# A network kernel of two blocks: the attention jobs of its last two layers start early and in another order, each with one dense tile beside it

## What is computed

```python
u = x * (1 + scale) + shift
h = split_cols(u @ w_in)                 # 27 feature tiles and 6 token tiles
o_dsa = dsa_mixer(rope(dsa_q), rope(dsa_k), dsa_v, rope(idx_q), rope(idx_k), idx_w)
o_fox = fox_mixer(fox_q, fox_k, fox_v, log_sigmoid(fox_f + b_f))
kc, vc = nsa_compress(...)               # silu(blocks @ w1) @ w2
o_nsa = nsa_mixer(nsa_q, rope(nsa_q), kc, vc, rope(ks), vs, rope(kw), vw, sigmoid(nsa_g))
mix = concatenate([o_dsa, o_fox, o_nsa])
y = (mix * silu(gate)) @ w_out
x = layer_norm(ALPHA * x + (1 + gate_c) * y, ln_g, ln_b)
```

## Time and profile before

| | |
|---|---|
| median of 3 runs | 1975.18 us (1973.48 to 1976.91) |
| span of the profiled execution, first to last instruction | 1978.9 us |
| mean granted PE clock in it | 0.944 |
| PE busy | 1833.1 us, 93% |
| DVE busy | 830.0 us, 42% |
| ACT busy | 393.5 us, 20% |
| moved by DMA | 480.10 MB, 243 GB/s on average |

### The profile page before, as it was taken

One profiled execution on the slowest core, in us unless ns is written; L12 is line 12 of the kernel. 1 busy time (PEld: TensorE's weight loads), 2 busy tenths in 40 slices (PEclk: granted clock), 3 DMA queues, 4 the chain that ended last, 5 costly groups with the idle time before them and its releaser, 6 DMA issues. The chain is left out here.

```text
span 1978.9 us, 41365 instructions
## 1 busy us (share of the span) xinstructions
PE 1833.1 (93%) x17309; PEld 1471.5 (74%) x17309; DVE 830.0 (42%) x2291; ACT 393.5 (20%) x1107; POOL 2.3 (0%) x6
## 2 busy tenths in 40 slices
PE   6999897999989987999999999998979998899987
PEld 4587675888878865799688887777658876688766
DVE  3766552678967913111110111111124755236651
ACT  3242333000014232000000000000022333113331
POOL 0000000000000000000000000000000000000000
PEclk7999998999999986999999999999979988899988
DMA  9632332799982141999999999999962411234000
GB/s 393 230 127 86 128 130 104 293 364 351 373 340 107 64 170 63 420 419 411 367 419 418 383 379 351 420 419 418 413 265 107 192 65 64 89 125 179 35 1 22
DMA packets 67902, 480.10 MB, mean 243 GB/s; under 512 B 7425, under 2 KB 9729, under 8 KB 9857
## 3 DMA queue, kind: packets, MB, share of 16 engines
q1 hardware_dynamic: 67712, 477.40, 60.9%
HBM read 476.32 MB, written 1.05 MB: 241 GB/s over the span
## 5 line engine op out<-in xcount | busy, mean ns | idle before, releaser
L523 PE MATMUL PS<-sb_U,sb_ring 128*128 128x256 f32 (+1 forms) x1456 | 378.1, 418 | 15.2 <-PEq L253 9.7
L523 PEld LDWEIGHTS PS<-sb_U,sb_ring 128*128 128x128 f32 x1456 | 285.0, 199 | 96.2 <-issue 58.8
L523 PE MATMUL PS<-sb_arena 128*64 128x128 f32 (+9 forms) x884 | 157.3, 356 | 7.8 <-DVE sb_arena L760 4.0
L798 PE MATMUL PS<-sb_U,sb_ring 128*128 128x256 f32 x704 | 156.4, 385 | 4.1 <-PEq L253 4.1
L798 PEld LDWEIGHTS PS<-sb_U,sb_ring 128*128 128x128 f32 x704 | 135.2, 193 | 25.3 <-issue 6.9
L523 PEld LDWEIGHTS PS<-sb_arena 64*128 64x128 f32 (+4 forms) x884 | 111.0, 179 | 47.8 <-issue 26.2
L379 DVE SCALAR_TENSOR_TENSOR sb_arena<-sb_ring,sb_cs,sb_arena 128x256 f32<-128x256 f32 x280 | 135.8, 485 | 10.0
L1778 PE MATMUL PS<-sb_ring,sb_arena 128*64 128x256 f32 x1008 | 129.1, 384 | 0.6 <-ACT sb_arena L2031 0.6
L523 PE MATMUL PS<-sb_YT,sb_ring 128*128 128x256 f32 x512 | 124.9, 399 | 3.5 <-ACT sb_YT L686 1.5
L1720 PE MATMUL PS<-sb_arena,sb_ring 128*64 128x98 f32 (+3 forms) x3072 | 121.3, 238 | 1.0 <-ACT sb_arena L2031 0.6
L1720 PEld LDWEIGHTS PS<-sb_arena,sb_ring 128*64 128x64 f32 x3072 | 116.1, 136 | 8.0 <-issue 5.7
(11 more groups left out here) (358 smaller groups left out, 2062.5 us busy)
## 6 DMA issues: line engine op xcount, KB each, us to landing
sb_ring<-stream SPq DMA_DIRECT2D x370, 1024.0 KB, 9.3
sb_arena<-stream SPq DMA_DIRECT2D x80, 1024.0 KB, 15.6
sb_consts<-consts SPq DMA_DIRECT2D x1, 1774.5 KB, 26.6
sb_U<-ctxT SPq DMA_DIRECT2D x1, 1024.0 KB, 6.5
sb_XT<-xT SPq DMA_DIRECT2D x1, 1024.0 KB, 8.4
out<-sb_XT SPq DMA_DIRECT2D x8, 128.0 KB, 2.0
sb_small<-small SPq DMA_DIRECT2D x1, 292.0 KB, 2.8
sb_consts<-consts SPq DMA_DIRECT2D x1, 129.0 KB, 2.7
```

Of the source, the lines that this page charges most:

```text
L523: ins = pe.transpose(o, l, r) if t.turn else pe.matmul(o, l, r, start=s, stop=e)
L798: ins = pe.matmul(PS[:, m % 4, h * T:(h + 1) * T], w[:, h, kt, :], src[:, kt, :], start=(kt == 0), stop=(kt == KT - 1))
```

## The change

The change replaces the code around the job loop by a small language of names, and the tables with it. In each late layer:

- The jobs run in another order: fox 0 and 1 (places 0 to 3), all of nsa (4 to 15), fox 2 (16, 17), dsa (18 to 21). The filling before place 0 shrinks to t2, qi0, ki, qf0, kf0, their ropes, and the first two forgetting biases. t0, kc, qf1, kf1, vc, sg2, c0, ks, c1, t1, c2, c3, qn0, kw and sg3 stand in places 0 to 3, three to seven units to a place; from place 4 on each place has one dense tile, but place 10 and places 19 to 23 have none. Before, places 2, 5, 8, 18 and 20 to 23 had none.
- Names ahead of the bar come before `turn_probs`, those behind it after. `ix` is the next index head, `find` the next search, `~x` the rope of x, `fb` a forgetting bias. The second half of the index heads stands two to a place in places 7 to 10; all eight searches stand in places 11 to 17, one to a place and two in place 17.
- Two activations of the filling become Tanh with a DVE operation behind (the gates of nsa, the silu of the compression).
- Areas move: the sums of the compression lie in YT, the residual at 1536, the squares for its norm at 4096. The order of the stream's units follows the new order of the tiles.
- The output tiles stay one pass after the last job, written anew as `out_last`.

```diff
-L2_UNITS = ("qi0", "qi1", "ki", "kw", "t2", "", "kc", "vc", "t1", "", "c0", "", "ks", "small", "c1", "", "qn0", "qn1", "c2", "", "c3", "",
...
-L2_BESIDE = ("t0", "t1", "", "qf0", "kf0", "", "qf1", "kf1", "", "qf2", "kf2", "sg2", "kd", "sg3", "qd0", "sg4", "qd1", "sg0", "", "sg1",
-             "", "", "", "")
+L2_UNITS = ("t2", "", "qi0", "ki", "qf0", "kf0", "t0", "", "kc", "qf1", "kf1", "vc", "sg2", "ks", "c0", "", "c1", "", "t1", "",
...
+L2_JOBS = [("fox", m, t) for m in range(2) for t in range(2)] + [("nsa", h, t) for h in range(6) for t in range(2)] + \
+    [("fox", 2, t) for t in range(2)] + [("dsa", m, t) for m in range(2) for t in range(2)]
+L2_FRONT = "t2.0 t2.1 small_cols qi0 forget1 ki ~qi0 forget2 qf0 ~ki forget3 kf0 fb0 fb1"
+L2_BESIDE = ("t0.0 t0.1 | kc ix", "qf1 kf1 ix | fb2 fb3 vc ix", "sg2 c0 ix | ks c1 ix",
+             "t1.0 t1.1 c2 ix | c3 qn0 ~ks ix whole kw ~qn0 sg3 second ~kw ix", "qn1 | ~qn1", "qi1 |", "sg5 | ~qi1", "qn2 | ix ix ~qn2",
+             "kd | ix ix", "sg6 | ix ~kd ix", "| ix ix", "qd0 | find", "sg7 | find ~qd0", "qf2 | find", "kf2 | find fb4 fb5", "qd1 | find",
+             "sg4 | find ~qd1", "sg0 | find find", "sg1 |", "|", "|", "|", "|", "|")
...
-            rs = area(4096, KT * T).rearrange("p (k t) -> p k t", k=KT)
+            rs = area(1536, KT * T).rearrange("p (k t) -> p k t", k=KT)
...
-            sums = wk.rearrange("p j n -> p (j n)").rearrange("p (z f n) -> p z f n", z=2, f=2)
+            sums = YT[:, 5:7, :].rearrange("p k (f n) -> p k f n", f=2)
...
-                return add(None, matmuls, "act", lambda act, bank, link: nc.scalar.activation(hc[:, 0:2 * NC], bank[:, 0:2 * NC], ACT.Silu), needs)
+                raw = add(None, matmuls, "act", lambda act, bank, link: nc.scalar.activation(hc_th[:, 0:2 * NC], bank[:, 0:2 * NC], ACT.Tanh, scale=0.5),
+                          needs)
+                raw.release = add(None, None, "dve", lambda dve, bank, link: dve.scalar_tensor_tensor(
+                    out=hc[:, 0:2 * NC], in0=hc_th[:, 0:2 * NC], scalar=1.0, in1=bank[:, 0:2 * NC], op0=ALU.add, op1=ALU.mult), (), after=(raw,),
+                    peek=raw)
+                return raw.release
...
-                return add(None, None, "dve", f, (compressed,), serial=True)
+                return add(None, None, "dve", f, (), serial=True)
...
-            for j in range(4):
-                summed.append(half_sum(j // 2, j % 2, built[j]))
-                index_heads(2)
...
+                tanh = add(None, None, "act", lambda e, b, link: nc.scalar.activation(ng, ng, ACT.Tanh, scale=0.5), (cols_in,))
+                add(None, None, "dve", lambda e, b, link: e.tensor_scalar(ng, ng, 0.5, 0.5, ALU.mult, ALU.add), (tanh,))
...
-            order = [("nsa", h, t) for h in range(6) for t in range(2)] + [("fox", m, t) for m in range(3) for t in range(2)] + \
-                    [("dsa", m, t) for m in range(2) for t in range(2)]
...
+            def beside(names):
+
+                for name in names.split():
+                    if name[0] == "~":
+                        x = raws[name[1:]]
+                        made[name] = roped(x, qr_nsa[:, int(name[3]), :] if name[1:3] == "qn" else x, r32 if name[2] == "i" or name[1:] == "ki" else r64,
+                                           made[name[1:]])
+                    elif name[:2] in ("t0", "t1", "t2"):
...
+                    elif name == "ix":
+                        t, h = heads.pop(0)
+                        index_head(t, h, made["iw"], made["~ki"], made[f"~qi{h // 4}"])
+                    elif name == "find":
+                        search(*finds.pop(0))
...
+            for i, names in enumerate(L2_BESIDE):
+                early, later = names.split("|")
+                if 0 <= i - 1 < len(L2_JOBS):
+                    softmax_scale(i - 1, jobs[i - 1])
+                if i < len(L2_JOBS):
+                    kind, x, t = L2_JOBS[i]
                     job = {"nsa": nsa_job, "fox": fox_job, "dsa": dsa_job}[kind](x, t)
-                    job["needs"] = {"nsa": (nsa_ready, kcT_ready), "fox": tuple(fox_in[2 * x:2 * x + 2]), "dsa": tuple(dsa_in)}[kind]
+                    job["needs"] = needs_of(kind, x)
                     jobs.append(job)
-                if 0 <= i - 1 < len(order):
-                    softmax_scale(i - 1, jobs[i - 1])
-                if i < len(order):
                     softmax_scores(i, job)
-                    softmax_exp(i, jobs[i])
-                if L2_BESIDE[i]:
-                    background(L2_BESIDE[i])
-                if 0 <= i - 1 < len(order):
+                    softmax_exp(i, job)
+                beside(early)
+                if 0 <= i - 1 < len(L2_JOBS):
                     turn_probs(i - 1, jobs[i - 1])
-                if i in (0, 2, 4, 6, 8):
-                    search(*((0, 3) if i == 0 else (1, i // 2 - 1)))
-                if i in (13, 15, 17):
-                    x, raw = dsa_raw.pop()
-                    dsa_in.append(roped(x, x, r64, raw))
-                if 0 <= i - 2 < len(order):
+                beside(later)
+                if 0 <= i - 2 < len(L2_JOBS):
                     weigh_values(i - 2, jobs[i - 2])
...
+            def out_last(k):
+
+                def matmuls(bank, chunk):
+                    w = chunk.rearrange("p (n k c) -> p n k c", n=2, k=KT)
+                    return [(bank[:, 0:T], w[:, k % 2, kt, :], YT[:, kt, :], kt == 0, kt == KT - 1) for kt in range(KT)]
+                return add(IN2_CH + CMP_CH + k // 2, matmuls, "dve", lambda dve, bank, link: dve.scalar_tensor_tensor(
+                    out=rs[:, k, :], in0=bank[:, 0:T], scalar=one_gate[:, k:k + 1], in1=XT[:, k, :], op0=ALU.mult, op1=ALU.add),
+                    (done["out", len(L2_JOBS) - 1],))
```

133 lines of the change are left out of this document (58 added, 75 removed).

## The result

| | before | after |
|---|---|---|
| median (4 runs each, beside one another) | 1976.05 us (1973.48 to 1984.80) | 1997.97 us (1993.05 to 2001.03) |
| ratio, 95% interval | | 1.0101 (1.0068 to 1.0134) |
| span of the profiled execution | 1978.9 us | 1993.1 us |
| mean granted PE clock | 0.944 | 0.944 |

The change makes the kernel about 22 us slower (13 to 26 by the interval). The forecast was slower by 10.8 us, 1986 us: the sign is right, the size is half, and the median lies 1 us above the range. By the ratio of runs taken side by side the change costs 20 us, which puts it at 1995 us from the 1975.2 us that the forecast starts from.

What follows compares the result with a forecast made beforehand. PE's work was taken to bound the filling, with PE's waits for DVE's scalings, lower clock and tail behind it. Two layers of +1.9 us plus tails of +4.3 and +2.7 us took 1975.2 to 1986 us, range 1967 to 1997.

Steps and rivals of the forecast that it cites:

- PE's work is the same: PE in the whole change: equal tiles, jobs and output pass, so nothing is added to the sum.
- The middle: Places 2 to 10: waits of 2.45 us go, 3.0, 0.6 and 0.8 us come; +1.9 us a layer.
- Place 17 and the tail: Last jobs up to the output: DVE late, PE waits 3.5 us at place 17; +4.3 and +2.7 us in the layers.
- The clock, equal: Lower-clock stretches behind bare places: as many microseconds lost after as before, 12.0 us in both layers.
- Tables, areas, stream: ACT's table loads, moved areas and new chunk order: zero each, as covered or adding no wait.
- The sum: Whole kernel: two layers of +1.9 us plus tails of +4.3 and +2.7 us, +10.8 us, giving 1986 us.
- The cover works: Rival at place 10 and the tail: DVE catches up, waits and clock losses shrink; 1968 us, chance 0.25.
- Nothing to measure: Rival: late scalings cost half, 5 us, and a lower-clock stretch of 3.4 us goes; 1977 us, chance 0.13.
- ACT's tables: Rival in the filling: four fewer table loads of 1.28 us were on the path; 1970 us, chance 0.02.
- Slower by more: Rival: forecast waits plus one more lower-clock stretch of 5.2 us a layer; 1996 us, within the slower side's 0.60.

Runs made afterwards that it cites:

- e13_fill10: Changed kernel with five unread products of constants on PE at bare place 10 alone, nothing in the tail: ratio 1.0072, median 1988.58 us.
- e1_pairs: Changed kernel with its ten single index heads paired, so all 16 a layer stand two by two: ratio 1.0094 to the kernel before.
- e2_find: Changed kernel with one of the two searches of place 17 moved to place 13: ratio 1.0085 to the kernel before.
- e3_fill: Changed kernel with unread products of constants on PE ahead of its waits at places 10, 18, 19, 20 and 22: ratio 1.0021, median 1982.96 us.
- e4_acts: Changed kernel with Silu and Sigmoid back in place of the two Tanh forms: ratio 1.0094 to the kernel before.
- e6_before_fill: Kernel before, with unread products of constants on PE where it waits for a scaling: ratio 0.9928, median 1964.65 us.
- e10_norm_fill: Kernel before with products of constants in its scaling waits, plus five ahead of each late layer's first dense tile: ratio 0.9912, median 1962.37 us.
- e8_apart: Kernel before, with its eight pairs of index heads a layer parted by a tile, rope or compression product: ratio 1.0091.

## Why the prediction was right in its sign and half in its size

- *"PE's work is the same: equal tiles, jobs and output pass; the sum has nothing for it."* This is the step that failed. The instructions are equal, but not what they take. Three pairs of heads with 256 keys and two with 128 were parted in each layer: 3 x 0.68 + 2 x 0.47 = 3.0 us, as e13_fill10's rows show at the upper clock. Two layers: 6 us that the sum lacked. I had read two index heads, 0.70 us, from a row that held a pair, and used it for the two heads of place 9, which stand on either side of a rope and take 1.38 us. I did not ask what the heads that the tables put alone would take.
- *The middle, +1.9 us a layer.* Right. The turn of job 9 waits 2.62 us (3.0 forecast; the 0.7 us that the parted heads of place 9 hold PE back are in this difference, and e1_pairs, which pairs them, waits 3.21), the scores of place 4 0.28 (0.6), the rope of qn1 0.47 (0.8). At place 7 the same pattern gave 0.57 + 0.30 us, which I had missed. Together 4.24, less the 2.45 us that went: +1.8. That the total came out so near is partly luck: three waits were 1.0 us shorter than forecast, and the 0.9 us missed at place 7 made up for it.
- *Place 17 and the tail, +4.3 and +2.7 us.* Right, a little small. The wait is 4.19 us (3.5), the tail 28.3 us (27.6): +5.0 and +3.4. It was worked out from DVE's and ACT's stretches, one after the other, and e2_find confirms that the search stands in that chain: 1.94 us of search, 1.80 us of wait.
- *The clock, equal.* Right in the middle of the layers, 10.2 us where 12.0 were. That wait and clock are tied as I had said is shown by e3_fill and e13_fill10.
- *Tables, areas, stream.* Zero, as said: e4_acts for the tables; PE never waits for a transfer in the late layers.
- *The sum.* 10.8 forecast; with 6 for the heads, 1.4 for the tails and -2 for clock and middle it is 16, and the stages of the two profiles give 17.6. The medians say 22; 16 and 17.6 lie inside the interval of 13 to 26, so the rest is not told apart from chance. Beside the heads each term held within 1 us a layer.
- *The rivals.* "The cover works" counted on DVE's free time, and DVE was late at exactly the places where its list had been filled. "Nothing to measure" and "ACT's tables" did not happen. "Slower by more" named the right number, 1996 us, by the wrong mechanism: more stretches at the lower clock, where it was PE's own work.

At full clock the difference is the same: e3_fill and e6_before_fill, changed and unchanged kernel with products in their waits, stand 18 us apart (1.0021 and 0.9928). What the change costs is therefore not clock, but heads and late scalings. Whether the moved areas or the order of the jobs by itself add something small was not tested apart from the tables.

## What to carry to other kernels

Equal instructions are not equal work: before moving small products apart, look in the timeline at what a neighbour gave them, and price them alone and in a pair. Where an engine works strictly in the order of a list, read its share of busy time between two deadlines and not over the stage; every search, rope or head that moves ahead of a scaling moves that scaling. And where PE must wait a microsecond or more just ahead of dense work, it can pay to give it useless products of the same length: 20 of them a layer made the kernel before 13.6 us faster. They must fit into the wait: in the second layer of e10_norm_fill they began late and delayed the work behind them.

## What I had not expected of the hardware

- Useless products in PE's waits made both kernels faster: by 0.7% before, by 15 us after the change. In the changed kernel nearly all of the gain up to the output pass came from a single pause of 2.6 us a layer.
- The clock fell with PE busy throughout, behind a row of small products: 3.00 us busy of 3.00 at 0.50 in e8_apart. The dense tile behind it took 3.0 us longer in the first layer and 1.7 us in the second.
- Two products with 32 rows each take 0.70 us on different quarters of the rows, 1.13 us on the same one, and 1.38 us apart.
- The tail, some 20 us in which another engine sets the pace, takes 19.85 us at 1.2 GHz and 19.06 us with PE at 2.4 GHz nearly throughout (0.50 and 0.91 granted).
